# Fused block, tile 1's last turns and first row pairs: repeat calls, two units of work and the order of pair sums moved

## The chip, the cores and the metric

The kernel runs on one core of one Trainium2 chip. The metric is the device time of one execution in microseconds; lower is better.

## The reference, cut to what matters

Two transformer blocks run one after the other on 256 tokens of width 1024. The first mixes tokens (a bidirectional retention and a differential attention, both with 4 heads, joined and projected by `w_out`) and then looks up experts: for each token and each of 8 heads it scores two sets of 128 sub-keys, takes the best 16 of each, the best 16 of their 256 sums, and gathers those experts' rows. The second block (short convolution, cross attention to a memory, gated feed-forward, block attention and so on) follows on the result. The part around the change, in the reference's words:

```python
x = x + mod[:, 2] * (jnp.concatenate([ret_lat, diff_lat], axis=-1) @ w_out[layer])
h2 = modulate(x, norm2_g[layer], mod[:, 3], mod[:, 4])
...
q = (hb @ w_query).reshape(t, PEER_HEADS, 2, PEER_HALF)
s = jnp.einsum('thpc,hpnc->thpn', q, sub_keys)
v1, i1 = lax.top_k(s[:, :, 0], PEER_TOPK); v2, i2 = lax.top_k(s[:, :, 1], PEER_TOPK)
best, pos = lax.top_k(cand, PEER_TOPK)          # cand = v1 + v2, 256 sums
gate = jax.nn.softmax(best, axis=-1)
act = jax.nn.gelu(jnp.einsum('thkd,td->thk', u, hb), approximate=False)
return jnp.einsum('thk,thkd->td', gate * act, vsel)
```

## The kernel before, in words

The 256 tokens are two tiles of 128. The experts' rows (the u half and the v half side by side, 2048 float32 to a row) come in 256 gathers, n = 0 to 255: a gather brings one row to each of the 128 partitions, 1.05 MB. Sixteen gathers are one group g = n // 16; groups 0 to 7 belong to tile 0 and 8 to 15 to tile 1. Group g of tile 0 is its head g, and its indices must be regrouped over partitions. There are nine places for rows (SLOTS = 9).

For each row DVE takes the dot product of u with the token (`dots`, line 2132). For each pair of rows (n0, n0 + 1) ACT then applies the gelu (L1580), multiplies by the gate (L1586) and writes two small diagonal weights (L1593), and PE adds the weighted v rows up (eight matmuls in the loop over `n0`, L1160, called the pair's sums here), which raises `v_used`. POOL issues the gathers (L1634): gather n waits until `v_used` says that row n-9 is out of its place. Each of the first ones also waits for the last use of the memory that its place had before: gather 4 for the turn at13, 5 for `diff_out`, 6 for the turn m11, 7 for the turn md1.

The dots need the token repeated over the partition groups. `repeat_tokens(t, g)` (line 782) makes that for g = 0 to 3 on PE, two PSUM units each (e00a, e00b and so on, L789), and `repeat_copy` (line 1373) brings it out on ACT (L1206). Pair 0 needs g = 0 and 1, pair 2 needs 2 and 3.

Four PSUM banks are handed round as units in one fixed order, the list `UNITS` (line 278); each unit names the engine that empties it (D is DVE, A is ACT), and a unit opens only when the one four places ahead is empty. A turn is a block of PE transposes to a bank of its own (`turn_blocks`, L699): at10 to at13 turn tile 1's attention weights, mr1 and md1 turn the retention and the attention output of tile 1 ahead of the output projection, and `mix_turn` copies them out, mr1 on ACT (L1341, four copies) and md1 on DVE (L1919).

The table `PICK_WORK` (line 183) says what PE does ahead of the sums of pair n0: `out 0` and `out 1` are the two halves of tile 1's output projection (L746, 16 matmuls each), `query q02` a query projection (L769, it needs the weight block wq 1), `keys 02` its sub-key scores (L779), `regroup 1` the matmul that spreads group 1's indices (L796). ACT's table `after` (line 1449) and DVE's `first` (line 2173) say what these engines do behind the pair: in `first` the entry j stands behind the dots of rows 2j and 2j + 1. `half_top`, `best_pairs`, `next_pairs`, `pair_rows` and `spread` are DVE's steps from key scores to a group's indices; `select(g)` (L2071) reads the regrouped ones, after which POOL may gather the group; `residual_out(1)` (L1960, L1962) reads both halves of the output projection.

Weights come through SP's queue into four places of a ring, 2.1 MB a block. The block wq 1 goes into the place of `out 0`'s weights and is issued when half 0 of tile 1's projection has read them (`out_half_used`); wq 2 follows when half 1 is done. SP issues in one order and waits for each place.

Of the kernel before, what the change touches and what calls it, by code (L numbers as in the profile page):

```python
# [19 lines left out]
D = 1024  # L20
# [157 lines left out]
def regroup_at(c):  # L178
# [1 line left out]
    return 112 if c == 8 else 16 * (c - 1) + 2  # L180


PICK_WORK = {2: ["out 0"], 4: ["out 1"], 6: ["regroup 1", "query q02"], 8: ["keys 02", "query q03"], 10: ["keys 03"], 16: ["h2_turns 1"],
# [95 lines left out]
for _e, _names in (("D", "nx c4x0"), ("A", "c4x1"), ("D", "c4k0"), ("A", "c4k1 c3x0 c3x1 c0x0"), ("D", "c0x1"), ("A", "c0k"), ("D", "r8 r9"),  # L279
# [5 lines left out]
    UNITS += [(n, _e) for n in _names.split()]  # L285
for _n in sorted(PICK_WORK):
    for _w in PICK_WORK[_n]:
# [34 lines left out]
def build_program(nc, a, out):  # L322
# [5 lines left out]
    with ExitStack() as ctx:  # L328
# [5 lines left out]
        def sem(name):  # L334
            if name not in sems:
                sems[name] = ctx.enter_context(nc.semaphore(name))
            return sems[name]
# [272 lines left out]
        def _(pe):  # L610
# [98 lines left out]
            def diff_turn(t, h):  # L709

                pe.wait_ge(probs_ready, 4 * t + h + 1)
                turn_blocks(turn(f"at{t}{h}"), [EX[t][:, h % 2, 0, j * P:(j + 1) * P] for j in range(4)])

            def diff_values(t, h):

                turned(turn(f"at{t}{h}"))
                for j in range(4):
                    v = PC[:, j, 1280 + h * P:1280 + (h + 1) * P] if j < 2 else PR[:, j - 2, 2560 + h * P:2560 + (h + 1) * P]
                    m = mm(M[1][:, h * P:(h + 1) * P], aT[:, h % 2, j], v, start=(j == 0), stop=(j == 3))
                m.then_inc(diff_out, 1)  # L720
# [61 lines left out]
            def repeat_tokens(t, g):  # L782

                if t:
                    pe.wait_ge(dots_done, 125 + g)
                for half in range(2):
                    b = open_unit(f"e{t}{g}" + "ab"[half])
                    for q in range(4):
                        m = mm(b[32 * q:32 * q + 32, :], ident[:, 32 * g:32 * g + 32], h2[:, t, half * 512:(half + 1) * 512], start=True, stop=True)  # L789
                    m.then_inc(unit_ready, 1)  # L790
# [151 lines left out]
            key_scores(0, 1)  # L942
            diff_turn(1, 2)
            diff_values(1, 1)
            diff_turn(1, 3)
            diff_values(1, 2)
            regroup(0)
            diff_values(1, 3)
            repeat_tokens(0, 0)
            repeat_tokens(0, 1)  # L950
            pe.wait_ge(sem("mix_ret"), 2)
            turn_blocks(turn("mr1"), [PR[:, 1, c * P:(c + 1) * P] for c in range(4)])
            pe.wait_ge(sem("mix_diff"), 2)
            turn_blocks(turn("md1"), [PR[:, 1, 2048 + c * P:2048 + (c + 1) * P] for c in range(4)])
            repeat_tokens(0, 2)
            repeat_tokens(0, 3)

            def key_block(l, i, half, b):

# [225 lines left out]
        def _(act):  # L1185
# [133 lines left out]
            def out_squares(k, acc, wait):  # L1319
                act.wait_ge(*wait)  # L1320
                for h in range(4):
                    q = f(junk[:, h * P:(h + 1) * P], acc[:, h * P:(h + 1) * P], ACT.Square, accum_out=yss[:, 4 * k + h:4 * k + h + 1])
                q.then_inc(sem("ysum"), 1)

            def out_root(k):
                act.wait_ge(sem("yms"), k + 1)
                f(ysd[:, 4 * k:4 * k + 4], yms[:, 4 * k:4 * k + 4], ACT.Sqrt).then_inc(sem("ysd"), 1)
# [5 lines left out]
            def mix_turn(kind, t):  # L1333
                n = turn(kind + str(t))
                if n % 2 == 0:
                    return
                act.wait_ge(turn_ready, n + 1)
                for c in range(4):
                    k = c if kind == "mr" else 4 + c
                    sc = cols[:, C_RN + c:C_RN + c + 1] if kind == "mr" else gd[:, c:c + 1]  # L1340
                    q = f(mixT[t][:, k], T[1][:, c * P:(c + 1) * P], ACT.Copy, scale=sc)  # L1341
                q.then_inc(turn_free[1], 1)
# [24 lines left out]
            def gate_exp(g):  # L1367
                b = g % 4
                act.wait_ge(sem("best_ready"), g + 1)
                f(comb[:, b, 1], best4[:, 16 * b:16 * b + 16], ACT.Exp, bias=nbest4[:, b:b + 1],  # L1370
                  accum_out=pz4[:, b:b + 1]).then_inc(gate_exp_done, 1)

            def repeat_copy(t, g):

                for half in range(2):
                    name = f"e{t}{g}" + "ab"[half]
                    if UNITS[unit(name)][1] == "A":
                        unit_copy(name, h2g[g][:, half * 512:(half + 1) * 512])

            def h2_square(t):  # L1380
                act.wait_ge(x_ready, 2 * (t + 1))
                f(h2[:, t], x[:, t], ACT.Square, accum_out=h2_ss[:, t:t + 1]).then_inc(sem("h2_sum"), 1)

            def h2_root(t):
                act.wait_ge(sem("h2_ms"), t + 1)
                f(h2_sd[:, t:t + 1], h2_ms[:, t:t + 1], ACT.Sqrt).then_inc(sem("h2_sd"), 1)

            def query_copy(name, wait=None):
                h = int(name[-1])
                whole = len(name) == 2  # L1390
                dst = qT[:, h % 2] if whole else qT[:, h % 2, :, int(name[1]) * P:(int(name[1]) + 1) * P]
                act.wait_ge(unit_ready, unit(name) + 1)
                for w in wait or ():
                    act.wait_ge(unit_ready, unit(w) + 1)
                w = 2 * TOK if whole else 2 * P
                f(dst, bank[unit(name) % 4][:, 0:w].rearrange("p (s n) -> p s n", s=2), ACT.Copy).then_inc(unit_free["A"], 1)
# [19 lines left out]
            diff_exps(1, 3)  # L1416
            diff_copy(1, 2)
            out_root(2)
            out_squares(3, M[1], (diff_out, 8))
            out_root(3)  # L1420
            repeat_copy(0, 0)
            repeat_copy(0, 1)
            mix_turn("mr", 1)
            repeat_copy(0, 2)
            repeat_copy(0, 3)

# [19 lines left out]
            def g5_move():  # L1446
                f(g5row, g5early, ACT.Copy).then_inc(sem("g5_moved"), 1)

            after = {2: [lambda: gate_exp(1)], 6: [lambda: query_copy("q02", ("k00",))], 8: [lambda: h2_square(1), lambda: query_copy("q03", ("k01",))], 10: [lambda: h2_root(1)],
                     14: [lambda: gate_exp(2)],  # L1450
                     16: [lambda: h2_turn(1)], 18: [lambda: query_copy("q10")], 20: [lambda: query_copy("q11")],
                     22: [lambda: query_copy("q12", ("k10",))], 24: [lambda: query_copy("q13", ("k11",))],
# [187 lines left out]
        def _(dve):  # L1640
# [271 lines left out]
            def mix_turn(kind, t):  # L1912
                n = turn(kind + str(t))
                if n % 2:
                    return
                dve.wait_ge(turn_ready, n + 1)
                k = 0 if kind == "mr" else 4
                g = cols[:, C_RN:C_RN + 4] if kind == "mr" else gd
                tt(mixT[t][:, k:k + 4], T[0][:, :].rearrange("p (c n) -> p c n", c=4), g.unsqueeze(2).to_broadcast([P, 4, P]),  # L1919
                   ALU.mult).then_inc(turn_free[0], 1)  # L1920
# [34 lines left out]
            def residual_out(t):  # L1955

                for half in range(2):
                    c = slice(half * 512, (half + 1) * 512)
                    name = f"o{t}" + "ab"[half]
                    tt(gated[t][:, c], unit_in(name)[:, :], g2row[:, c], ALU.mult).then_inc(unit_free["D"], 1)  # L1960
                    copied(name)
                    tt(x[:, t, c], x[:, t, c], gated[t][:, c], ALU.add).then_inc(x_ready, 1)  # L1962
# [200 lines left out]
            def memory_scale(l):  # L2163
# [4 lines left out]
                for k in range(KC):  # L2168
# [1 line left out]
                    q = stt(memT[l][:, k], memT[0][:, k], cols[:, g:g + 1], rs_m, ALU.mult, ALU.mult)  # L2170
                q.then_inc(sem("mem_scaled"), 1)

            first = [[lambda: mix_turn("md", 1), lambda: half_top(1, 0), lambda: half_top(1, 1)], [lambda: best_pairs(1), lambda: next_pairs(1)],
                     [lambda: pair_rows(1, 0), lambda: pair_rows(1, 1), lambda: spread(1)], [lambda: residual_out(1), lambda: select(1)], [], [lambda: h2_mean(1), lambda: key_copy(0, 2), lambda: half_top(2, 0), lambda: half_top(2, 1)],
                     [lambda: h2_apply(1), lambda: best_pairs(2), lambda: next_pairs(2)],
                     [lambda: key_copy(0, 3), lambda: pair_rows(2, 0), lambda: pair_rows(2, 1), lambda: spread(2)]]
            then = {(1, 0): [lambda: h2_turn(1)], (1, 1): [lambda: late_row(0), lambda: late_row(1), lambda: key_copy(1, 0), lambda: key_copy(1, 1)],
# [215 lines left out]
```

## Time and profile before

| What | Value |
|---|---|
| Median of 3 runs | 1727.83 us (1727.57 to 1728.28) |
| The profiled execution | 1727.59 us, its span 1725.8 us |
| PE busy | 1522.8 us, 88% |
| DVE busy | 752.1 us, 44% |
| ACT busy | 502.5 us, 29% |
| POOL busy | 290.8 us, 17% |
| Moved by transfers | 586.83 MB, 340 GB/s over the span |
| Chain that ended last | PE 70%, DMA 19%, DVE 6% |

Busy shares are means over stages that differ, so they are read beside the forty slices, the stretches and the chain. Times in rows are microseconds from the start of the span; a matmul's end is modelled. The granted clock of TensorE is given as a share of its full 2.4 GHz, 0.5 being 1.2 GHz.

### The profile page before, as it was taken

What the parts mean: (1) busy time and instruction counts of PE and PEld (TensorE: products, weight loads), DVE (VectorE), ACT (ScalarE), POOL (GpSimd) and SP (SyncE); (2) the same over time, 40 slices, a digit from 0 to 9 for tenths busy, and PEclk for the clock granted to TensorE, in tenths of its full rate; (3) what the DMA queues carried; (4) which work ended last, traced back from release to release, by engine and by line L of the source; (5) the groups of instructions that cost most, each with busy time, mean ns of one, the idle gap of its engine ahead of it and who ended that gap; (6) DMA issues with size and microseconds to landing.
All of it is one profiled execution on the core that took longest, in us unless ns stands there. A gap on an engine that the chain in (4) does not pass through costs nothing.

```text
span 1725.8 us, 15582 instructions
## 1 busy us (share of the span) xinstructions
PE 1522.8 (88%) x5474; PEld 729.0 (42%) x5474; DVE 752.1 (44%) x1816; ACT 502.5 (29%) x1284; POOL 290.8 (17%) x264
## 2 busy tenths in 40 slices
PE   7999998695479895897999887899999999999998
PEld 3444463462144541333343333343344444455443
DVE  3753167966786566456334346532312100031101
ACT  3411224332433223324434224433411110122210
POOL 0000003433433343222222213321000000000000
PEclk9999998897589897898999998899999999999999
DMA  9645438999999999999999999999886677855775
GB/s 372 216 159 196 170 110 347 420 421 421 421 395 421 421 421 420 410 421 421 417 422 420 421 421 421 412 421 422 346 302 242 249 296 283 314 212 220 291 297 187
DMA packets 93869, 586.83 MB, mean 340 GB/s; under 512 B 6880, under 2 KB 7008, under 8 KB 28128
## 3 DMA queue, kind: packets, MB, share of 16 engines
q1 hardware_dynamic: 55920, 313.19, 46.4%
q0 software_dynamic: 37440, 270.55, 38.0%
q10 hardware_dynamic: 432, 2.10, 0.3%
q8 instruction: 44, 0.72, 0.2%
q14 instruction: 33, 0.27, 0.0%
HBM read 584.76 MB, written 1.05 MB: 339 GB/s over the span
## 4 chain that ended last, share of the span: by engine, by line
PE 70%; DMA 19%; DVE 6%; issue 2%; ACT 2%; POOL 0%; SPq 0%; POOLq 0%; DVEq 0%; ACTq 0%
PE bank L999 34%; DMA arena<-in_peer_rows,pidx 10%; PE bank L1077 7%; DMA ring<-in_weights 7%; PE bank L691 7%; PE bank L1160 5%; PE bank L964 2%; PE bank L769 2%; DVE arena L2132 2%; PE bank L975 2%; PE bank L1006 2%; PE bank L746 2%; DMA spare<-in_peer_rows,pidx 1%; PE bank L1059 1%; PE bank L661 1%
## 5 line engine op out<-in xcount | busy, mean ns | idle before, releaser
L1634 POOL DMA_INDIRECT arena<-in_peer_rows,pidx x227 | 255.6, 1126 | 582.3 <-PE bank L1160 533.9
L2132 DVE SCALAR_TENSOR_TENSOR arena<-arena,ring 128x1024 f32<-128x1024 f32 x227 | 273.3, 1223 | 111.7 <-DMA arena<-in_peer_rows,pidx 109.2
L999 PE MATMUL bank<-ring,arena 128*128 128x512 f32 x736 | 319.4, 593 | 0.0
L999 PE MATMUL bank<-ring,hT_all 128*128 128x512 f32 x544 | 244.5, 605 | 16.3 <-issue 10.6
L1160 PE MATMUL bank<-arena,keep 128*32 128x512 f32 x908 | 159.8, 702 | 103.3 <-ACT keep L1593 103.2
L999 PEld LDWEIGHTS bank<-ring,arena 128*128 128x128 f32 x736 | 138.5, 190 | 168.8 <-issue 168.7
L999 PEld LDWEIGHTS bank<-ring,hT_all 128*128 128x128 f32 x544 | 102.8, 193 | 151.6 <-issue 141.1
L1580 ACT ACTIVATE pf<-pf 128x2 f32<-128x2 f32 x128 | 25.9, 202 | 400.0 <-DVE arena L2132 366.5
L2253 DVE TENSOR_TENSOR x_all<-x_all,bank 128x512 f32<-128x512 f32 x40 | 27.5, 688 | 209.0 <-PE bank L1077 115.1
L1160 PEld LDWEIGHTS bank<-arena,keep 128*32 128x32 f32 x908 | 21.2, 115 | 171.5 <-ACT keep L1593 134.7
L691 PE MATMUL bank<-ring,hT_all 128*128 128x512 f32 x192 | 84.3, 594 | 0.6 <-DVE hT_all L1712 0.6
L1634 POOL DMA_INDIRECT spare<-in_peer_rows,pidx x29 | 32.7, 1129 | 298.0 <-DVE pidx L2055 207.1
L1077 PE MATMUL bank<-ring,arena 128*128 128x512 f32 x176 | 75.9, 592 | 0.0
L2276 DVE SCALAR_TENSOR_TENSOR arena<-bank,stat,arena 128x256 f32<-128x256 f32 x22 | 10.6, 484 | 136.2 <-ACT arena L1538 136.2
L1593 ACT ACTIVATE keep<-keep,pf 128x32 f32<-128x32 f32 x256 | 68.3, 314 | 4.2
L1077 PE MATMUL bank<-ring,s_all 128*128 128x512 f32 x128 | 58.5, 611 | 5.9 <-DMA ring<-in_weights 5.9
L964 PE MATMUL bank<-mem_all,ring 128*128 128x256 f32 x256 | 62.9, 404 | 0.0
L1586 ACT ACTIVATE pf<-pf,grouped 128x1 f32<-128x1 f32 x256 | 61.4, 287 | 4.4
L769 PE MATMUL bank<-hT_all,ring 128*128 128x128 f32 (+1 forms) x384 | 60.4, 316 | 0.8 <-ACT hT_all L1193 0.8
L975 PE MATMUL bank<-ring,mem_all 128*128 128x512 f32 x128 | 60.0, 617 | 0.0
L769 PEld LDWEIGHTS bank<-hT_all,ring 128*128 128x128 f32 x384 | 54.8, 196 | 9.2 <-issue 5.7
L964 PEld LDWEIGHTS bank<-mem_all,ring 128*128 128x128 f32 x256 | 50.8, 203 | 18.0 <-issue 9.2
(389 smaller groups left out, 1701.1 us busy)
## 6 DMA issues: line engine op xcount, KB each, us to landing
ring<-in_weights SPq DMA_DIRECT2D x122, 2048.0 KB
ring<-in_w_mod SPq DMA_DIRECT2D x12, 2048.0 KB
ring<-in_w_in SPq DMA_DIRECT2D x6, 2048.0 KB
ring<-in_weights SPq DMA_DIRECT2D x8, 1024.0 KB
ring<-in_weights SPq DMA_DIRECT2D x8, 512.0 KB
arena<-in_peer_rows,pidx POOLq DMA_INDIRECT x227, 15.4
mem_all<-in_b_mod POOLq DMA_DIRECT2D x3, 512.0 KB, 7.0
hT_all<-in_xT ACTq DMA_DIRECT2D x1, 1024.0 KB, 6.2
```

What stands on the lines that cost most here:

```text
L691: m = mm(b[:, :], src[:, k, t * P:(t + 1) * P], slot8[w][:, k], start=(k == 0), stop=(k == KC - 1))
L746: m = mm(bank[unit(f"o{t}" + "ab"[half]) % 4][:, :], mixT[t][:, k], slot4[w][:, k % 4, half * 512:(half + 1) * 512], start=(k == first), s ...
L769: m = mm(b[:, s * n:(s + 1) * n], slot8[w][:, k, c:c + P], hT[:, k, cols_of], start=(k == 0), stop=(k == KC - 1))
L964: m = mm(bk[:, b * TOK:(b + 1) * TOK], slot8[w][:, k, (2 * half + b) * P:(2 * half + b + 1) * P], memT[l][:, k], start=(k == 0), stop=(k = ...
L975: m = mm(b[:, :], memT[l][:, 4 * part + k, t * P:(t + 1) * P], slot4[w][:, k, half * 512:(half + 1) * 512], start=(part == 0 and k == 0), ...
L999: m = mm(b[:, :], src[:, k], slot8[w][:, k], start=(k == 0), stop=(k == KC - 1))
L1077: m = mm(b[:, :], v.fT[k], slot8[w][:, k % 8], start=(k == ks[0]), stop=(k == ks[-1]))
L1160: m = mm(acc[b][r:r + 32, :], diag[n % 8], vslot[n % SLOTS][:, b * 512:(b + 1) * 512], start=(n % 128 < 4), stop=(n % 128 >= 124))
L1586: m = f(pw2[:, c + k:c + k + 1], pgel2[:, c + k:c + k + 1], ACT.Copy, scale=grouped[:, g % 4, i % 4, 1, i // 4:i // 4 + 1])
L1593: f(diag[n % 8], eq32, ACT.Copy, scale=pw2[:, c + k:c + k + 1]).then_inc(sem("diag_ready"), 1)
L1634: nc.gpsimd.indirect_dma_start(out=row_in[n % SLOTS], out_offset=None, in_=a["peer_rows"], in_offset=bass.IndirectOffsetOnAxis(ap=pidx[:, ...
L2132: stt(uslot[n % SLOTS], uslot[n % SLOTS], 1.0, h2g[n % 4], ALU.mult, ALU.mult, accum_out=pact2[:, 16 * (g % 2) + k:16 * (g % 2) + k + 1]). ...
```

## The change

PE makes repeat call 0 between the values of head 1 and the turn at13 instead of behind the last values, and calls 1 to 3 in one go ahead of the turns mr1 and md1. ACT copies repeat 0 ahead of the squares, the others in one go, and turns mr1 behind pair 0. Output projection half 0 moves from ahead of pair 2's sums to ahead of pair 4's, half 1 from pair 4's to pair 6's, and regroup 1 from pair 6's to pair 8's. On DVE every step of group 1 but the md1 turn moves one pair back, so that the dots of rows 2 and 3 come right behind those of 0 and 1. `UNITS` follows: e00a and e00b ahead of g0, and g1 behind q02.

```diff
     return 112 if c == 8 else 16 * (c - 1) + 2
 
 
-PICK_WORK = {2: ["out 0"], 4: ["out 1"], 6: ["regroup 1", "query q02"], 8: ["keys 02", "query q03"], 10: ["keys 03"], 16: ["h2_turns 1"],
+PICK_WORK = {4: ["out 0"], 6: ["out 1", "query q02"], 8: ["regroup 1", "keys 02", "query q03"], 10: ["keys 03"], 16: ["h2_turns 1"],
              18: ["regroup 2", "query q10"], 20: ["row r10", "row r11", "keys 10", "query q11"], 22: ["keys 11", "query q12"], 24: ["keys 12", "query q13"],
              26: ["keys 13", "query q4"], 28: ["keys 04", "keys 14"], 30: ["query q5"], 32: ["keys 05", "keys 15"],
              36: ["query q6"], 38: ["keys 06", "keys 16"], 42: ["query q7"], 44: ["keys 07", "keys 17"], 58: ["mean nm"]}
...
                    ("A", "s00a s00b c5x0"), ("D", "c5x1"), ("A", "s01a s01b c5k0"), ("D", "c5k1"), ("A", "s02a s02b"), ("D", "r4 r5 p00 p01"),
                    ("A", "s03a s03b"), ("D", "p02 p03"), ("A", "c1x0 c1x1"), ("D", "r6 r7"), ("A", "c1k0"), ("D", "c1k1"), ("A", "c2x0"),
                    ("D", "o0a o0b"), ("A", "c2x1 s10a s10b s11a s11b"), ("A", "q00"), ("D", "p10 p11 k00 p12 p13"),
-                   ("A", "s12a s12b q01"), ("D", "gfirst"), ("A", "s13a s13b"), ("D", "k01 g0"),
-                   ("A", "e00a e00b e01a e01b e02a e02b e03a e03b")):
+                   ("A", "s12a s12b q01"), ("D", "gfirst"), ("A", "s13a s13b"), ("D", "k01"), ("A", "e00a e00b"), ("D", "g0"),
+                   ("A", "e01a e01b e02a e02b e03a e03b")):
     UNITS += [(n, _e) for n in _names.split()]
 for _n in sorted(PICK_WORK):
     for _w in PICK_WORK[_n]:
...
             key_scores(0, 1)
             diff_turn(1, 2)
             diff_values(1, 1)
+            repeat_tokens(0, 0)
             diff_turn(1, 3)
             diff_values(1, 2)
             regroup(0)
             diff_values(1, 3)
-            repeat_tokens(0, 0)
             repeat_tokens(0, 1)
+            repeat_tokens(0, 2)
+            repeat_tokens(0, 3)
             pe.wait_ge(sem("mix_ret"), 2)
             turn_blocks(turn("mr1"), [PR[:, 1, c * P:(c + 1) * P] for c in range(4)])
             pe.wait_ge(sem("mix_diff"), 2)
             turn_blocks(turn("md1"), [PR[:, 1, 2048 + c * P:2048 + (c + 1) * P] for c in range(4)])
-            repeat_tokens(0, 2)
-            repeat_tokens(0, 3)
 
             def key_block(l, i, half, b):
 
...
             diff_exps(1, 3)
             diff_copy(1, 2)
             out_root(2)
+            repeat_copy(0, 0)
             out_squares(3, M[1], (diff_out, 8))
             out_root(3)
-            repeat_copy(0, 0)
             repeat_copy(0, 1)
-            mix_turn("mr", 1)
             repeat_copy(0, 2)
             repeat_copy(0, 3)
 
...
             def g5_move():
                 f(g5row, g5early, ACT.Copy).then_inc(sem("g5_moved"), 1)
 
-            after = {2: [lambda: gate_exp(1)], 6: [lambda: query_copy("q02", ("k00",))], 8: [lambda: h2_square(1), lambda: query_copy("q03", ("k01",))], 10: [lambda: h2_root(1)],
+            after = {0: [lambda: mix_turn("mr", 1)], 4: [lambda: gate_exp(1)], 6: [lambda: query_copy("q02", ("k00",))], 8: [lambda: h2_square(1), lambda: query_copy("q03", ("k01",))], 10: [lambda: h2_root(1)],
                      14: [lambda: gate_exp(2)],
                      16: [lambda: h2_turn(1)], 18: [lambda: query_copy("q10")], 20: [lambda: query_copy("q11")],
                      22: [lambda: query_copy("q12", ("k10",))], 24: [lambda: query_copy("q13", ("k11",))],
...
                     q = stt(memT[l][:, k], memT[0][:, k], cols[:, g:g + 1], rs_m, ALU.mult, ALU.mult)
                 q.then_inc(sem("mem_scaled"), 1)
 
-            first = [[lambda: mix_turn("md", 1), lambda: half_top(1, 0), lambda: half_top(1, 1)], [lambda: best_pairs(1), lambda: next_pairs(1)],
-                     [lambda: pair_rows(1, 0), lambda: pair_rows(1, 1), lambda: spread(1)], [lambda: residual_out(1), lambda: select(1)], [], [lambda: h2_mean(1), lambda: key_copy(0, 2), lambda: half_top(2, 0), lambda: half_top(2, 1)],
+            first = [[lambda: mix_turn("md", 1)], [lambda: half_top(1, 0), lambda: half_top(1, 1)], [lambda: best_pairs(1), lambda: next_pairs(1)],
+                     [lambda: pair_rows(1, 0), lambda: pair_rows(1, 1), lambda: spread(1)], [lambda: residual_out(1), lambda: select(1)], [lambda: h2_mean(1), lambda: key_copy(0, 2), lambda: half_top(2, 0), lambda: half_top(2, 1)],
                      [lambda: h2_apply(1), lambda: best_pairs(2), lambda: next_pairs(2)],
                      [lambda: key_copy(0, 3), lambda: pair_rows(2, 0), lambda: pair_rows(2, 1), lambda: spread(2)]]
             then = {(1, 0): [lambda: h2_turn(1)], (1, 1): [lambda: late_row(0), lambda: late_row(1), lambda: key_copy(1, 0), lambda: key_copy(1, 1)],
```

## Rows read from the trace of the kernel before

**Rows 1.** The page: transfers' busy tenths in 40 slices of 43 us.
```profile
DMA  9645438999999999999999999999886677855775
```
**Rows 2.** Stretches: us, busy (x instructions) of PE, PEld, DVE, ACT, POOL; clock, DMA share, GB/s.
```profile
261.00:283.00 22.00, 15.90 (x118) 8.25 (x116) 18.66 (x60) 13.70 (x39) 6.85 (x7) 0.86 1.00 413
283.00:287.00 4.00, 4.00 (x9) 1.82 (x6) 3.86 (x11) 3.21 (x6) 2.73 (x2) 0.50 0.49 141
...
291.00:295.00 4.00, 4.00 (x16) 1.32 (x15) 2.94 (x7) 0.89 (x4) 0.94 (x1) 1.00 0.53 131
295.00:301.00 6.00, 6.00 (x21) 2.14 (x19) 1.58 (x3) 0.33 (x2) 0.94 (x1) 1.00 1.01 426
301.00:330.00 29.00, 16.93 (x126) 10.94 (x122) 27.25 (x74) 12.19 (x31) 14.18 (x12) 0.82 1.01 421
```
**Rows 3.** The chain that ended last, in order of time: start, us, what.
```profile
281.24 1.94 PE bank L1160 x8
283.17 8.97 PE bank L746 x16
293.14 7.07 PE bank L746 x16
301.99 11.37 DMA arena<-in_peer_rows,pidx
...
383.19 17.52 DMA arena<-in_peer_rows,pidx
```
**Rows 4.** Timeline of POOL: gathers 7, 9, 11 and 27.
```profile
275.13 1.01 POOL L1634 DMA_INDIRECT arena<-in_peer_rows,pidx  x1 [2.57 <-PE bank L699]
...
283.96 0.94 POOL L1634 DMA_INDIRECT spare<-in_peer_rows,pidx  x1 [6.58 <-PE bank L1160]
...
293.93 0.94 POOL L1634 DMA_INDIRECT arena<-in_peer_rows,pidx  x1 [6.81 <-PE bank L1160]
...
339.82 0.94 POOL L1634 DMA_INDIRECT spare<-in_peer_rows,pidx  x1 [3.49 <-PE bank L1160]
```
**Rows 5.** Line L1634, gather 9 alone, then gather 27 alone: issue to landing.
```profile
DMA to landing us min/median/max: 5.5/5.5/5.5
...
DMA to landing us min/median/max: 8.3/8.3/8.3
```
**Rows 6.** Timeline of PE: the turn at13, two repeat calls, two turns, regroup 1, q02.
```profile
265.51 0.65 PE L699 MATMUL bank<-keep,arena 128*128 128x128 f32 x4 [2.79 <-DVE arena L1872]
...
269.54 3.80 PE L789 MATMUL bank<-h_all,keep 128*32 128x512 f32 x32
...
273.27 1.09 PE L699 MATMUL bank<-keep,arena 128*128 128x128 f32 x8
...
301.13 0.49 PE L796 MATMUL bank<-s_all,keep 128*128 128x128 f32 x2
...
301.45 3.78 PE L769 MATMUL bank<-hT_all,ring 128*128 128x128 f32 x32
```
**Rows 7.** Timeline of ACT: mr1's copies, the table load, pair 0's weights.
```profile
273.96 1.15 ACT L1341 ACTIVATE s_all<-bank,keep 128x128 f32<-128x128 f32 x4
...
278.61 1.28 ACT L1580 ACT_TABLE_LOAD   x1
...
280.65 0.53 ACT L1593 ACTIVATE keep<-keep,pf 128x32 f32<-128x32 f32 x2
```
**Rows 8.** Timeline of DVE: md1's copy, dot 2, the residual, the selection of group 1.
```profile
275.26 0.69 DVE L1919 TENSOR_TENSOR s_all<-bank,small 128x512 f32<-128x512 f32 x1
...
279.54 1.23 DVE L2132 SCALAR_TENSOR_TENSOR arena<-arena,ring 128x1024 f32<-128x1024 f32 x1
...
299.38 0.69 DVE L1960 TENSOR_TENSOR h_all<-bank,mem_all 128x512 f32<-128x512 f32 x1 [5.37 <-PE bank L746]
...
302.05 0.28 DVE L2071 TENSOR_TENSOR s_all<-bank,keep 128x128 f32<-128x128 f32 x1
```
**Rows 9.** Timeline of SP's queue: the block for q02.
```profile
292.18 8.45 SPq L601 DMA_DIRECT2D ring<-in_weights  x2
```

## The prediction

> **What bounds the kernel now.** The page comes first: the transfer engines' line of the forty slices stands at 9 from slice 7 to slice 27 [rows 1], so from about 295 to 1200 us the time is what the weights and the 256 row gathers take to arrive. The stretches around the change say where that river begins. Between 283 and 287 us and between 291 and 295 us it moves only 141 and 131 GB/s, against 426 in the next stretch [rows 2]: 4 x (1 - 141/424) + 4 x (1 - 131/424) = 5.4 us of transfer time is lost there for good, and the ceiling on what this change can win by filling them. The chain that ended last says why they are empty: PE's first sums at 281.24, then output projection half 0 (8.97 us), the second pair's sums, half 1 (7.07 us), and only then a gather that takes 11.37 us [rows 3]. POOL may issue gather n only when the sums of row n-9 are done, so gathers 9, 11 and 13 go out at 283.96, 293.93 and 301.99 [rows 3, 4]. Behind 302 us the limit changes hands: DVE is busy 27.25 of 29 us from 301 to 330 [rows 2], PE's queries follow, and the chain meets the gathers again at 383.19, where one needs 17.52 us because others stand ahead of it [rows 3].
>
> So two things must be asked: how much earlier the transfers run, and whether the engines' stretch from 302 to 383, which no transfer holds up, moves at all.
>
> **The repeats.** PE idles 2.79 us ahead of the turn at 265.51; two repeat calls take 3.80 us, so one call (1.9) fits into the gap [rows 6]. Its two copies on ACT then come ahead of the squares, and free their banks early. Behind the gap PE has three calls instead of two ahead of the turns mr1 and md1: it worked 269.54 to 273.27 on two and then 1.09 on both turns [rows 6]; now it ends near 269.6 + 5.6 + 1.1 = 276.3, or 275.3 if the filled gap keeps the clock up. I take 275.8. POOL's gather 7 waits for md1: about 277, not 275.13 [rows 4]. That costs nothing or some tenths: gathers 0 to 6 (1.05 MB each, 2.5 us at the 413 GB/s of 261 to 283 [rows 2]) cover until 278.5, and data follow an issue by 1.5 to 2 us.
>
> ACT's last repeat copy ends near 275.3 instead of 278.6, as four turn copies no longer stand among them; the table load of 1.28 us and the first pair's work end at 281.18 [rows 7], 3.3 us earlier: 277.9. Then come the four mr1 copies (1.15 us [rows 7]). DVE waits for md1 now, from about 274 to 275.8, turns it (0.69) and takes dots 2 and 3 (1.23 each, ends overlapping, 2.3 in all; the first began at 279.54 [rows 8]) from 276.6 to 278.9. ACT is free at 279.15, so the second pair's sums start at X = 280.5. The half tops (from 275.95 to 279.54) are only moved behind, and so are the pair steps: DVE's work up to dots 9 is 294.0 - 279.54 + 3.6 + 2.3 = 20.4 us from 276.6, done at 297, ahead of what it then waits for.
>
> **Sums 2 ahead of half 0.** PE's first sums took 1.94 us at the lower clock; the granted clock is 0.50 from 283 to 287, after PE had idled from 278 to 281, and 1.00 from 291 on [rows 2]. Half 0 took 8.97 us partly at that level and half 1 7.07 us at the upper [rows 3]. PE still has two short idle stretches, so I take 8.1 for half 0, bounds 7.1 and 9.0. It ends at R = 280.5 + 1.94 + 8.1 = 290.5 (288.6 to 291.5), against 292.14. Gather 9 goes out about 280.5, 11 about 283.3, 13 about R + 1.9 = 292.4, instead of 283.96, 293.93 and 301.99. By bytes: fifteen gathers of 1.05 MB and one weight block of 2.1 MB keep 424 GB/s busy from 261 to 303, the next block (released by half 1) to 308, gathers 15 and 16 to 313, and the next ones are out by then. Both holes close: 5.4 us of head.
>
> **Where the head is spent.** In the engines' stretch gather 27 goes out at 339.82 and lands in 8.3 us; the shortest landing of any gather, with the queue empty, is 5.5 [rows 4, 5]. With more than 8.3 - 5.5 = 2.8 us of head the queue runs dry there. So if the engines' stretch does not move, 2.8 us are left; if it moves by s (earlier is plus), min(5.4, 2.8 + s). The Trainium skill (DMA: Bandwidth & Descriptors, "Anatomy of one DMA") puts a transfer from GpSimd at 2.0 us plus bytes over 436 GB/s, 4.4 us here; by that 3.9 + s would be left and my sum would be 3.0 us of gain instead of 1.9. The trace has no gather under 5.5, so the row decides.
>
> **Whether the stretch moves.** It starts on DVE, at the selection of group 1 (302.05), which waits for PE's regroup 1 [rows 6, 8]. Before, regroup 1 stood ahead of query q02; now it stands behind q02 and behind the sums of rows 6 and 7. From R on: sums 1.0, half 1 7.1, q02 3.8 [rows 6], sums 1.0, and 0.9 from regroup to the selection (301.13 to 302.05): R + 13.8 + W, where W is a wait of q02 for its weights. DVE has dots 8 and 9 behind it by then (2.3 us), so the old equivalent is 302.05 + 2.3 = 304.35. s = 304.35 - R - 13.8 - W, and the gain is 293.35 - R - W.
> The wait removed (DVE idle 5.37 us ahead of 299.38 [rows 8]) comes back: about 2 us ahead of residual_out and 3 to 4 ahead of the selection.
>
> W: SP issues q02's block when half 0 is done, at 292.18 [rows 9], and q02 began at 301.45 without a wait, so landing took 9.3 us at most. From R that is 1.2 us behind half 1's end (R + 8.1); new is that gathers stand where the hole was, some 0.6 MB more, up to 1.5 us. Below, zero. I take W = 1.0 between 0 and 2.7: the row is an upper end.
>
> **Sum.** R = 290.5, W = 1.0: s = -0.95, gain 1.9 us. Bounds: 288.6 and 0 give 4.8; 291.5 and 2.7 give a loss of 0.8. The profiled execution took 1727.59, so 1725.7, and as the median of the runs is 0.24 above it, 1725.9. All else in the diff costs nothing: bank order changes but every bank is read by then (DVE's 3.5 us cover); gate_exp(1) moves with its group; keys and q03 only follow.
>
> **Rivals.**
> (a) *The whole hole.* The clock stays up through half 0 and q02's block lands in time: R = 288.6, W = 0, s near +2, gain 4.8 to 5.4, 1722.4 to 1723. For it: q02 never visibly waited, and PE has less idle time before half 0. Against it: the clock did fall after the idle time at 278 to 281. Chance 0.27.
> (b) *Equal shares.* If block and gathers take turns evenly, the block's last 1.6 MB go at 212 GB/s and land near R + 11.6; W = 3.5, loss 0.6, 1728.2. Against it: in the run before the block was alone until gather 11's data came near 295.5; evenly shared from there its last 1.5 MB would have landed near 302.6, and q02 started at 301.45. The Trainium skill (the same page, "Queues, rings and completion order") has each engine go round-robin between queue rows packet by packet, which is this case; the trace speaks against exactly even. Chance 0.14.
> (c) *Slower: q02's block last.* Place: PE ahead of q02. If the fourteen to fifteen gathers already out are served first, the block lands near 304, W about 5.4, PE stands idle that long, and the lower clock adds what it adds to the sums (1.94 for 1.06) and to the queries, about 1.9: W = 7.3 in effect, loss 4.5, about 1732. It decides from W = 3.3 as no gain and from 6.3 as slower by more than 0.2%. Against it: the block did overlap gather 11 before. Chance 0.14.
> (d) *The forecast*, gain 0 to 3.5: 0.45.
>
> A measurement of this kernel can tell about 0.2% (3.5 us) from no change. Faster by more: (a) and a corner of (d), 0.30. Slower: (c), 0.14. Within: 0.56. The range 1721.8 to 1729.5 takes in (a) with its ceiling of 5.4, (d), (b), and leaves most of (c) out.
>
> **What the new profile would show.** Right: a transfer line without the holes at 283 to 295; gather 9 near 280.5 and gather 11 near 283.3; gather 7 near 277; half 1 ending near 298.6; DVE's selection of group 1 at 305.3; gather 27 issued near 341 and landing in 5.5 to 6; the gather that met the chain at 383.19 landing some 2 us earlier. Wrong: a selection before 303.5 (then (a)), q02 starting 3 us or more after half 1 (then (b) or (c)), or holes that only moved, say to 305 to 312.

## The result, and the profile after

| What | Before | After |
|---|---|---|
| Median | 1727.32 us (6 runs, 1724.99 to 1728.28) | 1733.55 us (6 runs, 1732.08 to 1735.04) |
| Ratio to before | | 1.0040, 95% interval 1.0030 to 1.0051 |
| The profiled execution, its span | 1727.59, 1725.8 us | 1735.04, 1733.2 us |

The change makes the kernel 6.2 us slower. The forecast was 1.9 us faster with a range up to 1729.5. The time comes nearest to rival (c), told at 1732, but its mechanism is only a part of what happened. In what follows PE is TensorE, ACT ScalarE, DVE VectorE, POOL GpSimd and SP SyncE; R is the moment at which output projection half 0 ends.

The first part of the trace is nearly as predicted. This is the timeline of PE in the kernel after (start, us, instruction, its idle time before it in brackets):

```profile
263.31 1.92 PE L789 MATMUL bank<-h_all,keep 128*32 128x512 f32 x16
266.17 0.66 PE L699 MATMUL bank<-keep,arena 128*128 128x128 f32 x4 [0.94 <-DVE arena L1871]
...
269.19 5.36 PE L789 MATMUL bank<-h_all,keep 128*32 128x512 f32 x48 [0.35 <-DVE s_all L1984]
274.47 1.09 PE L699 MATMUL bank<-keep,arena 128*128 128x128 f32 x8
...
280.05 1.81 PE L1160 MATMUL bank<-arena,keep 128*32 128x512 f32 x8 [0.55 <-ACT keep L1592]
```

Repeat call 0 fills the gap that was 2.79 us [rows 6] and leaves 0.94; the turns end at 275.56 (forecast 275.8) and the second pair's sums start at 280.05 (forecast 280.5). Then the chain that ended last parts from the old one [rows 3]:

```profile
281.86 7.08 PE bank L746 x16
288.96 14.24 DMA ring<-in_weights
303.24 6.53 PE bank L769 x32
...
391.18 17.50 DMA arena<-in_peer_rows,pidx
```

Half 0 runs wholly at the upper clock and ends at 288.9 (forecast R = 290.5, best case 288.6). But the weight block that its end releases needs 14.24 us to land, where at most 9.3 had been seen before. PE and DVE show what that costs:

```profile
303.24 6.53 PE L769 MATMUL bank<-hT_all,ring 128*128 128x128 f32 x32 [6.26 <-DMA ring<-in_weights]
309.70 1.06 PE L1160 MATMUL bank<-arena,keep 128*32 128x512 f32 x8
```

```profile
311.22 0.29 DVE L2070 TENSOR_TENSOR s_all<-bank,keep 128x128 f32<-128x128 f32 x1 [11.82 <-PE bank L796]
```

PE stands idle 6.26 us ahead of q02, and q02 then takes 6.53 us instead of 3.78 [rows 6]. Behind it stand the sums of pair 6 and regroup 1, so DVE's selection of group 1 comes at 311.22 instead of 302.05 [rows 8], after 11.82 idle us. POOL waits as well: gather 15 needs the sums of pair 6.

```profile
291.95 0.94 POOL L1633 DMA_INDIRECT arena<-in_peer_rows,pidx  x1 [0.30 <-issue]
311.56 0.94 POOL L1633 DMA_INDIRECT arena<-in_peer_rows,pidx  x1 [18.67 <-PE bank L1160]
```

For almost 20 us no gather goes out (gather 15 went out at 307.02 before), and the transfer engines run dry. The stretches of the kernel after, with the columns of [rows 2]:

```profile
261.00:283.00 22.00, 17.88 (x133) 8.10 (x130) 18.90 (x60) 13.95 (x39) 10.21 (x11) 0.92 0.96 384
283.00:287.00 4.00, 4.00 (x10) 1.71 (x9) 3.83 (x12) 2.33 (x6) 2.14 (x2) 1.00 0.99 360
291.00:295.00 4.00, 4.00 (x10) 1.72 (x10) 3.69 (x11) 0.49 (x2) 1.58 (x2) 1.00 1.02 430
...
297.00:301.00 4.00, 0.00 (x0) 0.00 (x0) 2.33 (x4) 0.00 (x0) 0.00 (x0) 1.00 1.02 424
301.00:330.00 29.00, 16.40 (x106) 11.81 (x106) 17.84 (x52) 8.49 (x25) 7.88 (x8) 0.75 0.90 354
309.00:313.00 4.00, 4.00 (x35) 3.04 (x35) 1.60 (x4) 2.53 (x8) 0.97 (x2) 1.00 0.38 154
333.00:349.00 16.00, 12.92 (x71) 8.94 (x70) 14.17 (x40) 5.17 (x18) 5.45 (x6) 0.69 0.91 316
```

The old holes at 283 and 291 us are closed (360 and 430 GB/s instead of 141 and 131), as forecast. New ones stand at 309 to 313 and at 333 to 349, and DVE, which was busy 27.25 of the 29 us from 301 to 330, is busy 17.84. The stretch ahead, from 261 to 283, went down from 413 GB/s [rows 2] to 384. The bill by bytes, over equal stretches of before and after, follows. Before:

```profile
261.00:301.00 40.00, 33.90 (x166) 15.26 (x164) 30.71 (x91) 19.34 (x53) 11.57 (x11) 0.87 0.90 359
301.00:321.00 20.00, 13.22 (x110) 9.16 (x106) 18.66 (x52) 8.01 (x22) 12.00 (x10) 0.92 1.01 421
321.00:341.00 20.00, 13.30 (x72) 7.79 (x73) 17.89 (x51) 8.70 (x26) 5.00 (x5) 0.74 1.01 422
341.00:361.00 20.00, 20.00 (x156) 16.63 (x155) 15.91 (x38) 4.58 (x18) 7.71 (x7) 1.00 1.01 419
```

After:

```profile
261.00:301.00 40.00, 31.87 (x170) 13.50 (x166) 34.58 (x99) 19.35 (x53) 14.22 (x14) 0.96 0.98 398
301.00:321.00 20.00, 14.66 (x98) 11.65 (x98) 9.22 (x30) 6.82 (x18) 5.16 (x6) 0.83 0.86 338
321.00:341.00 20.00, 8.84 (x38) 3.54 (x39) 17.93 (x45) 8.28 (x25) 5.43 (x6) 0.54 0.95 364
341.00:361.00 20.00, 20.00 (x153) 16.17 (x152) 16.64 (x48) 4.57 (x18) 7.50 (x8) 0.95 0.94 347
```

From 261 to 301 us the mean went up from 359 to 398 GB/s, which is 39 x 40 / 421 = 3.7 us of transfers gained. The three stretches behind lose (83 + 58 + 72) x 20 / 421 = 10.1 us. That is 6.4 us net. It agrees with the bytes counted from the start of the span, 89.75 MB by 361 us for 92.56: 2.8 MB, or 6.7 of the 7.4 us between the two spans. Up to 0.66 us of this are not the change's: gather 0 already went out that much later (259.07 for 258.41), ahead of everything that was moved. Gather 27 goes out at 347.07 for 339.82 [rows 4], the gather on the chain at 391.18 for 383.19, and the last one lands at 1239.0 for 1230.9. So most of the loss is there by 361 us, less than one us comes behind it, and the work behind the last gather takes 0.7 us less than before.

### The profile page after: what moved, and what is told of

Same layout as the page of the kernel before. It is cut to its first block, busy times and chain, and to the rows that moved or that the text cites. A ratio compares the mean times of both kernels' runs of the same rounds, so it can differ in the third digit from the quotient of the medians.

```text
span 1733.2 us, 15582 instructions
## 1 busy us (share of the span) xinstructions
PE 1523.1 (88%) x5474; PEld 731.0 (42%) x5474; DVE 752.0 (43%) x1816; ACT 502.0 (29%) x1284; POOL 288.9 (17%) x264
## 3 DMA queue, kind: packets, MB, share of 16 engines
HBM read 584.76 MB, written 1.05 MB: 338 GB/s over the span
## 4 chain that ended last, share of the span: by engine, by line
PE 70%; DMA 18%; DVE 6%; issue 3%; ACT 2%; POOL 0%; SPq 0%; POOLq 0%; DVEq 0%; ACTq 0%
PE bank L999 34%; DMA arena<-in_peer_rows,pidx 11%; PE bank L1077 8%; PE bank L691 7%; DMA ring<-in_weights 7%; PE bank L1160 4%; PE bank L769 3%; PE bank L964 2%; DVE arena L2131 2%; PE bank L1006 2%; PE bank L975 1%; PE bank L746 1%; PE bank L1059 1%; PE bank L661 1%; PE bank L651 1%
## 5 line engine op out<-in xcount | busy, mean ns | idle before, releaser
L769 PE MATMUL bank<-hT_all,ring 128*128 128x128 f32 (+1 forms) x384 | 65.1, 333 | 7.0 <-DMA ring<-in_weights 6.3
L769 PEld LDWEIGHTS bank<-hT_all,ring 128*128 128x128 f32 x384 | 59.1, 211 | 15.8 <-DMA ring<-in_weights 7.1
```

Source lines behind the costliest of these rows:

```text
L769: m = mm(b[:, s * n:(s + 1) * n], slot8[w][:, k, c:c + P], hT[:, k, cols_of], start=(k == 0), stop=(k == KC - 1))
```

## The experiments

Times are in the order of the runs; the kernel before on the same chip stood at 1727.43 (e1 to e4), 1727.54 (e5 to e8) and 1728.16 us (e9, e10). Theory: the block of q02 lands late because gathers 9 to 12 (only 9 and 10 before) now go out ahead of half 0's end and share the transfer engines with it; PE's clock is lower behind its wait; q02, the sums and regroup 1 hang on it. Rivals: the moved repeats or DVE's order are what costs, or the order of PE's work alone.

**e1, the projection back.** The new kernel with the old place of both halves and of regroup 1:

```diff
-PICK_WORK = {4: ["out 0"], 6: ["out 1", "query q02"], 8: ["regroup 1", "keys 02", "query q03"],
+PICK_WORK = {2: ["out 0"], 4: ["out 1"], 6: ["regroup 1", "query q02"], 8: ["keys 02", "query q03"],
...
```

> The changed kernel, but projection half 0, half 1 and regroup 1 stand again ahead of the sums of pairs 2, 4 and 6; repeats, copies and DVE's later steps stay as changed. Theory A (the block of weights for q02 is late because half 0, which frees its place, now ends with four gathers already out): half 0 runs from about 280 to 287.5, the block is issued then with two gathers out and lands within 9.5 us, q02 waits under 1 us, and DVE's selection of group 1 starts near 300. Time 3 to 5 us under the kernel before. Theory B (DVE's steps of group 1 one pair later are what costs): still slower than before by some 3 us or more, whatever the block does. Theory C (the moved repeats, with gathers 7 and 8 later, cost): slower as well.

Measured: 1728.96 us, ratio 1.0009 (1.0000 to 1.0019). None of the three theories had this: the loss is mostly gone, against B and C, but the gain of A did not come. So the reordering of PE's work holds most of the loss, 4.6 of 6.2 us, and the repeats with DVE's order hold about 3 us at most and none that is clear of the noise. The profiled execution was one of its fastest (1725.54) and shows why:

```profile
287.02 11.72 DMA ring<-in_weights
```

The block lands in 11.72 us, not 14.24 (A had said 9.5, and a wait under 1 us); q02 waits 2.32 us and keeps the upper clock (3.84 us), the selection is at 298.80 and gather 27 at 336.89.

**e2, the repeats alone.** In addition ACT's `gate_exp(1)` and DVE's list are as before; what is left of the change is the repeat calls, their copies and mr1's copies behind pair 0.

```diff
-            first = [[lambda: mix_turn("md", 1)], [lambda: half_top(1, 0), lambda: half_top(1, 1)], [lambda: best_pairs(1), lambda: next_pairs(1)],
+            first = [[lambda: mix_turn("md", 1), lambda: half_top(1, 0), lambda: half_top(1, 1)], [lambda: best_pairs(1), lambda: next_pairs(1)],
...
```

> The kernel before with only the repeats, their copies and the turn copy of mr1 moved as in the change; the order of sums and DVE's order as before. Theory A: the first sums start near 278 instead of 281.2, half 0 ends near 288, and the time is 2 to 4 us under the kernel before. Theory C: no gain or slower, since the turns mr1 and md1 come later by 1 us and with them gathers 7 and 8. Theory B says as A, since DVE's order is the old one.

Measured: 1725.88 us, ratio 0.9993 (0.9983 to 1.0003): no loss, and no gain that can be told, so the outcome of theory C and not the 2 to 4 us of theories A and B. C's reason, late gathers, does not hold, though: its transfers are full from 261 to 301 us (415 GB/s for 359). In its profile q02 waits too, 3.83 us for a block that takes 13.24, and runs at the lower clock (6.26 us). On the same chip e2 lies 3.1 us under e1, from which it differs by DVE's list and the place of `gate_exp(1)` alone; in e7 and e8, the same two orders with PE kept busy, e7 is the faster one by 0.6 us, so that DVE's later steps cost anything is not shown.

**e3, gathers held until the block has landed.** The new kernel, with a wait on POOL ahead of gather 11:

```diff
+                if n == 11:
+                    pool.wait_ge(landed[slot_of[piece["wq", 1]]], 32 * (use_of[piece["wq", 1]] + 1))
```

> The changed kernel, but POOL issues gather 11 and all behind it only once the block for q02 has landed, so that only gathers 9 and 10 share the transfers with it. Theory A: the block lands by 295 to 296 instead of 303.2, q02 does not wait and runs at the upper clock, the selection of group 1 starts near 303 instead of 311, and the time is 2 to 5 us under the kernel before, so 8 to 11 under the changed one. Theory B: q02's wait goes, but the time stays above the kernel before by 2 us or more, as regroup 1 stands behind q02 and another pair's sums. A small hole in the transfers of about 1.5 us near 295 belongs to the edit.

Measured: 1728.19 us, ratio 1.0009 (0.9999 to 1.0018). This is the plainest evidence: 5.4 us come back though everything else of the change stands. Theory A's 2 to 5 us under the kernel before did not come, nor theory B's 2 us or more above it. From its chain:

```profile
291.53 7.81 DMA ring<-in_weights
```

With no gather behind 10 out, the same block lands in 7.81 us. In this execution half 0 took 8.86 us, partly at the lower clock, so gathers 9 and 10 had moved all their bytes when the block was issued (11.52 MB, eleven gathers) and it had the engines to itself; q02 has no wait (299.39 to 303.2) and the selection is at 304.67. It wins nothing over before, since the engines are not filled meanwhile (291 to 295 us: 184 GB/s) and gather 11 goes out only at 300.12.

**e4, e6: the clock kept up.** Matmuls on constants, written to a bank of turns, between half 1 and q02; 13 in e4, 8 in e6:

```diff
+                if name == "q02":
+                    turned(turn("md1"))
+                    for _ in range(8):
+                        mm(T[0][:, 0:444], ident, keep[:, K_EQ:K_END], start=True, stop=True)
```

> The changed kernel with 13 matmuls of 444 columns that nothing reads put ahead of q02 on PE, about 5.5 us of work in its wait of 6.3. If the lower clock behind the wait is part of the loss, q02 takes 3.8 us instead of 6.5 and the time is 2 to 3 us under the changed kernel, still 3 to 4 above the kernel before. If the transfers set the stretch behind it anyway, the time stays that of the changed kernel.

> As e4, with 8 matmuls instead of 13: 0.745 us each by e4's row, so 6.0 us in a wait of 6.26, where 13 took 9.7 and came 3.4 us too long. Theory clock: q02 starts near 303.3 and takes 3.8 instead of 6.5 us, the selection of group 1 starts near 308.5 instead of 311.2, and the time is 2 to 3 us under the changed kernel. Rival: the transfers behind it set the pace, and the time stays within 1 us of the changed kernel.

Measured: e4 1737.03 us (1.0058, 1.0042 to 1.0075). The 13 took 9.69 us and so delayed q02 themselves, which spoils the comparison; and though its last gather landed at 1239.0 as in the new kernel, the rest of that execution took 3 us longer, which stays unexplained. e6: 1731.44 us (1.0023, 1.0013 to 1.0033), 2.1 us less than the new kernel, though the two intervals still touch. Its block took 14.56 us, but q02 3.84 instead of 6.53, and the selection came at 307.4. The lower clock's share of the loss is thus near 2 us, as the theory of the clock had it.

**e5, regroup 1 ahead of q02.** Half 1 and regroup 1 ahead of pair 6's sums, q02 behind them:

```diff
-PICK_WORK = {4: ["out 0"], 6: ["out 1", "query q02"], 8: ["regroup 1", "keys 02", "query q03"],
+PICK_WORK = {4: ["out 0"], 6: ["out 1", "regroup 1"], 8: ["query q02", "keys 02", "query q03"],
...
```

> The changed kernel with regroup 1 ahead of the sums of rows 6 and 7 and query q02 behind them, so that the selection of group 1 and gathers 15 and 16 no longer stand behind the wait for the block. Theory A (the late block sets DVE's stretch in any case, since key_copy(0, 2) waits for q02 and its scores): the selection starts near 299, DVE then waits at the key copy until about 311, and the time is 1 to 4 us under the changed kernel, still 2 us or more above the kernel before. Theory B (what costs is that the selection stands behind q02): 5 to 7 us under the changed kernel, level with the kernel before or faster.

Measured: 1730.40 us (1.0017, 1.0007 to 1.0027); 3.1 us come back, as theory A had it, and not the 5 to 7 of theory B. Neither selection nor gather 15 waits for the block now (299.0, 298.65), yet the block takes 13.86 us, q02 waits 4.65 and takes 6.69, and gather 27 goes out at 343.69. So q02 has a way of its own to the end, through its copy and the keys, beside the selection's.

**e7, e8: the two good orders with a warm clock.** e1 with 4 and e2 with 5 of e6's matmuls.

> e1 with 4 of these matmuls (3.0 us) in q02's wait of 3.7. e1's runs lay between 1724.1 and 1730.8. If that spread is q02 behind its wait at the upper clock in some executions and at the lower in others, all runs come to lie near e1's lowest, 1724 to 1727, and the median 2 to 3 us under the kernel before. If the spread has another source, median and spread stay as in e1.

> e2 with 5 of these matmuls (3.7 us) in q02's wait of 4.3. In e2 q02 took 6.3 us behind its wait. Theory clock: q02 takes 3.8, everything behind it comes 2.5 us earlier, and the time is 3 to 5 us under the kernel before. Rival: the gathers' own arrival sets the stretch, and the time stays that of e2, about 1 us under the kernel before.

Measured: e7 1726.25 us (0.9991, 0.9981 to 1.0000), e8 1726.82 (0.9994, 0.9984 to 1.0003). e7 lies 2.7 us under e1, e8 0.9 above e2, where its rival had it; only the first speaks for the clock. The executions of e7 spread from 1724.3 to 1729.1, less than e1's but beyond the 1724 to 1727 of the expectation, so the clock at q02 is at most a part of e1's spread. Neither is faster than before by what can be told, and the 2 to 5 us expected did not come. e8 shows why a filled hole pays so little. Its stretches:

```profile
261.00:301.00 40.00, 35.48 (x191) 16.68 (x190) 36.17 (x102) 19.15 (x53) 12.39 (x13) 1.00 1.00 410
301.00:321.00 20.00, 12.18 (x93) 7.43 (x92) 15.03 (x43) 8.00 (x22) 8.87 (x8) 0.83 1.01 416
321.00:341.00 20.00, 15.47 (x83) 9.83 (x84) 17.89 (x51) 8.58 (x26) 5.82 (x6) 0.66 0.98 390
341.00:361.00 20.00, 20.00 (x151) 16.52 (x150) 15.01 (x38) 4.58 (x18) 7.12 (x7) 1.00 0.99 404
```

51 x 40 / 421 = 4.8 us are gained up to 301, and (5 + 32 + 15) x 20 / 421 = 2.5 us given back up to 361, where the engines let the gathers out too late: 2.4 us are left, and its span is 2.4 us under before's.

**e9, e10: how many gathers stand ahead of the block.** As e3, but gather 11 (e9) or gather 12 (e10) waits only until half 0 is done, when the block is issued too:

```diff
+                if n == 11:
+                    pool.wait_ge(sem("out_half_used"), 1)
```

> The changed kernel, in which GpSimd holds gather 11 (and all behind it) only until half 0 of the output projection is done, so that it goes out together with the weight block of query q02, not ahead of it (in the changed kernel at 282.75, six us earlier). Theory (the block shares the transfer engines with the gathers that are already out, and each one less lets it land sooner): two gathers, 9 and 10, are ahead instead of four, as in the kernel with the projection moved back, where the block took 11.72 us: here 11.5 to 12 us instead of 14.24; TensorE waits 3.5 to 4 us for it instead of 6.26; DVE's selection of group 1 near 308 instead of 311.2; transfers full until then; 1729.5 to 1731.5. Rival (the transfers work off everything in the order of its bytes, and holding gathers until landing helped only because the engines were left half empty): the block takes 14 us again and the time is within 1 us of the changed kernel's 1733.5. Second rival (what the block gains the late gathers lose, dots 11 and 12 then being late): the block lands in 11.7 us but the time stays above 1732.

> The same with gather 12 held until half 0 is done, and gather 11 let go ahead of the block as in the changed kernel. Theory (each gather that is out ahead of the block costs it about the same): three gathers out, between the run with two and the changed kernel with four: the block takes about 13 us, TensorE waits about 5 us, the selection comes near 309.8, 1731 to 1733. Rival (only the number of bytes asked for in all counts, or none of it matters): no difference to the changed kernel in any of these, 14.2 us and 1733.5.

Measured: e9 1730.57 us (1.0014, 1.0003 to 1.0024), e10 1732.28 us (1.0029, 1.0017 to 1.0040). The times are in order (2.4 us above the kernel before, 4.1, and 6.2 for the new kernel) and inside the theory's ranges; e9 is clear of the new kernel, e10's interval overlaps with it. From the chains of e9 and of e10:

```profile
291.60 9.91 DMA ring<-in_weights
```

```profile
287.56 13.55 DMA ring<-in_weights
```

In e9's profiled execution half 0 ran partly at the lower clock (8.83 us) and ended 2.6 us later than the new kernel's. All bytes of gathers 9 and 10 had been moved by then, which fits with a block of 9.91 us and not the 11.5 to 12 expected. The selection comes 15.2 us behind the end of half 0 in e9, 20.3 in e10 and 22.3 in the new kernel. Of e10's 2.0 us the block brings 0.7 (13.55 for 14.24); the rest is q02, 5.21 us for 6.53, again with the clock.

**What a block does among gathers.** The queues' rows of the trace give the mechanism: q1 is SP's queue with the weights, q0 POOL's with the gathers; packets, MB, share of 16 engines. Before, 294 to 298 us:

```profile
q1 hardware_dynamic: 191, 1.56, 96.1%
```

The new kernel, 289 to 292 us, then 294 to 302:

```profile
q0 software_dynamic: 170, 1.25, 98.8%
...
q1 hardware_dynamic: 221, 1.72, 51.3%
q0 software_dynamic: 227, 1.68, 50.2%
```

Two things add up. While both queues have work, they share evenly: 1.72 and 1.68 MB in 8 us, so 2.1 MB take 9.8 us; e3's block, by itself, needed 6.1 from its first packet to its last. And the block, issued at 288.96, moved nothing in the 3 us behind that: the gathers ahead had 98.8% of the engines. Its first packet starts 3.5 us after its issue; before, with the engines empty, it was 1.0 us. 292.4 + 9.8 is 302.2, and the block has landed at 303.2. The Trainium skill (DMA: Bandwidth & Descriptors, "Queues, rings and completion order") has the engines go round-robin between queues packet by packet. The trace agrees once both are being served; the 3 us at the start are not in that rule.

How long it takes goes by the bytes that are still to be moved when the block is issued, not by the number of gathers ahead. The MB outstanding are 1.05 for each gather issued, less what q0 has moved by then; the third column is the time from the block's issue to its first packet, each from the one profiled execution of a run:

| Run | MB outstanding | First packet | Landing |
|---|---|---|---|
| e3, no gather behind it | 0.0 | 1.0 us | 7.8 us |
| e9 | 0.0 | 1.0 | 9.9 |
| before | 0.0 | 1.0 | 9.3 at most |
| e1, e7 | 1.1, 1.2 | 2.4, 2.5 | 11.7, 12.5 |
| e2, e8 | 1.3, 1.6 | 2.8, 3.0 | 13.2, 14.0 |
| e10 | 1.9 | 3.5 | 13.6 |
| e5, new kernel, e6 | 2.7, 2.8, 3.0 | 3.4, 3.5, 3.5 | 13.9, 14.2, 14.6 |

All runs of the first five lines have the same two gathers, 9 and 10, ahead of the block, and it takes them 7.8 to 14.0 us. With more than 1.9 MB outstanding neither column grows by much. So the block does not wait for all that was queued before it: in the new kernel 1.3 of the 2.8 MB were still to come when its first packet moved. Why the delay stops at 3.5 us, no run shows. That a block is late does not cost by itself either: e8's takes 14.0 us, but it is issued at 285.43 and has landed by 299.5, and nothing is lost.

## Why the prediction was wrong

- **The repeats, the first sums, R: right.** First sums 277.85 (forecast 277.9), second pair's 280.05 (280.5), half 0's end 288.9 (290.5, inside its bounds); both holes closed. e1 and e2 show the same start, and that this part alone costs nothing that can be told. Only gather 7's delay (276.34 for 275.13), taken as free or some tenths, seems to have cost more: from 261 to 283 us the transfers lose 29 x 22 / 421 = 1.5 us, up to 0.66 of it by gather 0. Of the 5.4 us of head 3.7 were there at 301.
- **W, q02's wait for its weights: the term that failed.** Taken as 1.0 between 0 and 2.7, measured 6.26, and 2.75 more for q02 at the lower clock, for which the sum had no term. The reason given was that the block takes 9.3 us at most, and 1.5 us for 0.6 MB more of gathers. But the 9.3 us had been measured in the hole itself: before, the block moved 1.56 MB from 294 to 298 with no gather byte beside it. Whoever fills a hole must first ask what used it; the one user was the transfer that the next stage waits for. The mechanism stood in the rivals, each in part and each with a chance of 0.14: (c)'s gathers that go first hold for the first 3.5 us, (b)'s even shares for the rest.
- **The argument against rival (b): the misreading behind it.** It took gather 11's data as coming from 295.5, concluded that an even share would have made q02 late, and so held the trace to be against even shares. Gather 11's bytes came only from 298 on, 4 us after its issue, when 0.4 MB of the block was left; the row said nothing on shares. From 298 to 300, where both moved, the kernel before has 0.47 MB of gathers and 0.38 MB of the block, which is nearly even. The price of (b) alone, W = 3.5, was too low by 2.7 us, as the block's first packet came 3.5 us after its issue and not 1.0; it put the landing at R + 11.6, and it came at R + 14.3. Rival (c) had 5.4 us idle and 1.9 for the clock, 7.3 in all, against 6.26 + 2.75 = 9.0 measured. By the prediction's own formula the gain ends at W = 2.85, not at 3.3; nothing hangs on it.
- **s (how far the engines' stretch moves) and the head: the formula failed below zero.** With the measured terms s = 304.35 - 288.9 - 13.8 - 9.0 = -7.4; the selection itself, at 311.22 where 304.35 would have kept the pace, gives -6.9. By min(5.4, 2.8 + s) the loss would be 4.1 to 4.6 us; the profiled spans differ by 7.4. The formula lets 2.8 us of head make up for a part of a late stretch, and they were not there: POOL stood still from 292.9 to 311.56 behind the late sums of pair 6, gather 27 again had others ahead of it and took 7.9 us (8.3 before [rows 5]), and it landed at 355.0 for 348.1, 6.9 us later, which is s alone. Where the engines' stretch does not come late, a part of the head is kept, as the formula says: e8 kept 2.4 of 4.8 us.
- **That the selection starts the stretch: half right.** Gather 27 went out 34.3 to 34.6 us after q02's end in before, e1, e2 and e5, whether the selection was 3 or 10 us ahead of that end (e7 and e8: 35.6 and 35.4), and 36.4 to 37.3 us after it in the new kernel, e4, e6, e9 and e10, where regroup 1, the selection and dots 8 and 9 (2.3 us) come behind it. Only e3, which held its gathers, has more (41.5). So in all but e3 it is q02's end that goes with the stretch; the forecast reached it only by way of the selection.
- **"All else costs nothing": not contradicted,** and bounded by e1 (about 3 us at most) and by e2.

Open: the profiled execution of e1 is 2.1 us under before's by span, its median 1.5 us over before's; its executions spread from 1724.1 to 1730.8. Which of them fall to the lower clock at half 0 or at q02 one profile cannot tell. Nor was it tried to let the block go out earlier: its place in the ring is only free when half 0 is done.

## What to carry to other kernels

Before filling a hole in the transfers, look at which queue moves bytes in it and who waits for those: a landing time measured in a hole is not one to count on once the hole is filled. Here the block took 9.8 us for its bytes beside gathers where it took 6.1 by itself, plus up to 2.5 us more until its first packet, in which gathers queued before it went; the fewer bytes were outstanding at its issue and beside it, the sooner it landed (14.2 us with 2.8 MB outstanding, 11.7 with 1.1, 9.9 with none, 7.8 with none and no gather until it is in). And the sums that free a gather's place should not stand behind work that waits for a weight block: in e5, where regroup 1 and the sums went ahead of q02, 3.1 us came back.

## What the runs showed of the hardware

- The same 2.1 MB block from SP's queue landed in 7.8 us with the gathers held, in 9.9 with none outstanding but some issued behind it (e9), and in 11.7 to 14.6 us with 1.1 to 3.0 MB of gathers outstanding (e1, e2, e5 to e8, e10, the new kernel).
- Its first packet moved 1.0 us after its issue with nothing outstanding (before, e3, e9), 2.4 to 3.0 us with 1.1 to 1.6 MB, and 3.4 to 3.5 us with 1.9 to 3.0 MB.
- Two queues with work shared the engines evenly, 51.3% to 50.2% over 8 us; by itself the block of before moved 1.56 MB in 4 us, 96.1%.
- A gather's first byte can be late as well: gather 11 of before, issued at 293.93 beside the running block, moved nothing until 298.
- 6.26 us of idle PE cost 2.75 us in the next 32 matmuls: the granted clock in the new kernel is still 1.00 from 297 to 301 us, where PE does nothing, and then

```profile
303.00:307.00 4.00, 3.76 (x17) 3.76 (x18) 0.00 (x0) 0.00 (x0) 0.00 (x0) 0.50 1.02 426
```

the lower of its two levels (1.2 GHz) while q02 runs. In e6, whose PE idled only 0.61 us there, the clock was 1.00 and q02 took 3.84.
